# Three buffers instead of four for the raw weight panels of a two-layer trunk

## What is computed

```python
for layer in range(2):
    mod = silu(c) @ w_ada[layer] + b_ada[layer]            # six modulation vectors, for latents and context
    p = modulate(rms_norm(x, norm1), shift1, scale1) @ w_in[layer]
    y_m = mLSTM in both directions, context first, then latents
    y_a = grouped attention with 2-D rotary, latents see context and latents
    y_c = B * conv3(C * u)
    merged = sum over b of sigmoid(gate_b) * (y_b @ w_proj_b)
    x = x + g1 * (merged @ w_out)
    x = x + g2 * (relu(modulate(rms_norm(x, norm2), shift2, scale2) @ w_up) ** 2 @ w_down)
    # the context goes through the same, except behind the projections of the last layer
return rms_norm(x_latents) * final_norm
```

## Time and profile before

| | us |
|---|---|
| median of 3 runs | 1849.48 (1849.16 to 1849.73) |
| the profiled execution: its time | 1851.07 |
| the profiled execution: its span | 1849.3 |
| PE busy in the span | 1819.4 |
| DVE, ACT, POOL busy | 1051.0, 688.7, 156.6 |
| mean granted clock of TensorE | 0.997 |

### The profile page before, as it was taken

How to read it: one execution, slowest core, us unless ns; L and a number is a source line. 1 busy time by engine, 2 the same in 40 slices (tenths; PEclk the granted TensorE clock), 3 DMA queues, 4 the chain that set the end, 5 groups by cost and what they waited for, 6 DMA issues and landing times.

```text
span 1849.3 us, 24538 instructions
## 1 busy us (share of the span) xinstructions
PE 1819.4 (98%) x10027; PEld 1544.7 (84%) x10027; DVE 1051.0 (57%) x1544; ACT 688.7 (37%) x948; POOL 156.6 (8%) x159
## 2 busy tenths in 40 slices
PE   7999999999999999999999999999999999999998
PEld 4787788778888888878888888788998899999997
DVE  5435634544556665567675645655546656566555
ACT  3424434323222222243232323343644434445444
POOL 2100100001110101320000000301100110020000
PEclk9999999999999999999999999999999999999999
DMA  9221122121443453626444436132232375575653
GB/s 325 98 91 46 38 88 66 60 69 46 137 143 131 137 176 120 220 77 204 136 137 137 160 118 196 56 132 92 62 122 91 115 228 183 183 228 165 194 188 114
DMA packets 214271, 245.51 MB, mean 133 GB/s; under 512 B 5820, under 2 KB 186384, under 8 KB 214160
## 3 DMA queue, kind: packets, MB, share of 16 engines
q1 hardware_dynamic: 213856, 243.85, 40.8%
q10 hardware_dynamic: 304, 0.10, 0.0%
HBM read 242.89 MB, written 1.05 MB: 132 GB/s over the span
## 4 chain that ended last, share of the span: by engine, by line
PE 93%; DVE 2%; ACT 2%; issue 1%; POOL 0%; DVEq 0%; ACTq 0%; POOLq 0%
PE pp L1163 19%; PE pp L1167 19%; PE pp L1164 19%; PE pp L1172 4%; PE pp L1170 4%; PE pp L1171 4%; PE pc L1356 3%; PE pc L1408 2%; PE pp L1094 2%; PE pp L1095 2%; PE pp L1096 2%; PE pc L1053 2%; PE pc L1055 2%; PE pc L1054 2%; PE pc L1446 1%; PE pc L1423 1%
## 5 line engine op out<-in xcount | busy, mean ns | idle before, releaser
L1883 DVE TENSOR_TENSOR wL<-raw,wH 128x1024 fp32r<-128x1024 f32 (+1 forms) x360 | 452.5, 1298 | 238.6 <-ACT wH L1460 235.6
L1163 PE MATMUL pp<-hH,wH 128*128 128x512 f32 (+1 forms) x1708 | 571.1, 345 | 0.3 <-ACT hH L1668 0.3
L1164 PE MATMUL pp<-hH,wL 128*128 128x512 f32 (+1 forms) x1708 | 561.0, 339 | 0.0
L1460 ACT ACTIVATE wH<-raw 128x1024 fp32r<-128x1024 f32 x360 | 360.3, 1049 | 305.8 <-PE pp L1172 103.3
L1167 PE MATMUL pp<-hL,wH 128*128 128x512 f32 (+1 forms) x1708 | 439.7, 339 | 0.9 <-POOL hL L1856 0.6
L1163 PEld LDWEIGHTS pp<-hH,wH 128*128 128x128 f32 x1708 | 324.1, 190 | 43.4 <-issue 9.0
L1164 PEld LDWEIGHTS pp<-hH,wL 128*128 128x128 f32 x1708 | 324.3, 190 | 35.8 <-issue 1.7
L1167 PEld LDWEIGHTS pp<-hL,wH 128*128 128x128 f32 x1708 | 294.7, 190 | 36.7 <-POOL hL L1856 0.8
L1163 PE MATMUL pp<-yH,wH 128*128 128x512 f32 (+1 forms) x320 | 115.4, 367 | 0.0
L1170 PE MATMUL pp<-yH,wH 128*128 128x512 f32 (+1 forms) x320 | 114.4, 358 | 0.0
L1171 PE MATMUL pp<-yL,wH 128*128 128x512 f32 (+1 forms) x320 | 114.4, 358 | 0.0
(11 more groups left out here) (269 smaller groups left out, 2226.0 us busy)
## 6 DMA issues: line engine op xcount, KB each, us to landing
raw<-in_w_in SPq DMA_DIRECT2D x84, 1024.0 KB, 5.2
raw<-in_w_up SPq DMA_DIRECT2D x32, 1024.0 KB, 5.5
raw<-in_w_down SPq DMA_DIRECT2D x32, 1024.0 KB, 5.1
pair_W<-in_w_ada SPq DMA_DIRECT2D x10, 2048.0 KB, 8.0
ada_Y<-in_w_ada SPq DMA_DIRECT2D x10, 1024.0 KB, 11.9
ada_H<-in_w_ada SPq DMA_DIRECT2D x8, 1024.0 KB, 11.1
raw<-in_w_proj_m SPq DMA_DIRECT2D x8, 1024.0 KB, 5.1
raw<-in_w_proj_a SPq DMA_DIRECT2D x8, 1024.0 KB, 5.2
```

The costliest lines, as they stand in the source:

```text
L1163: pe.matmul(dsts[b], wh[b], hi[:, kt, ts_], start=first, stop=False)
L1164: pe.matmul(dsts[b], wl[b], hi[:, kt, ts_], start=False, stop=False)
L1460: act.activation(wH[:, p % HIGH, a:a + KH, :], raw[:, p % RAW, a:a + KH, :], ACT.Copy).then_inc(wH_ready, 1)
L1883: dve.tensor_tensor(wL[:, p % RAW, ks, :], raw[:, p % RAW, ks, :], wH[:, p % HIGH, ks, :].bitcast(F32), ALU.subtract).then_inc(wL_ready, 1)
```

## The change

The number of raw buffers goes from four to three.

```diff
-RAW = 4
+RAW = 3
```

## The result

The changed kernel takes 1856.6 us (median of 7 executions, 1854.34 to 1860.09), the kernel before 1849.73 (7 executions, 1848.45 to 1850.82). The ratio is 1.0041, with a 95% interval from 1.0031 to 1.0050: slower, by 5.7 to 9.2 us. The forecast was 1857.2. The profiled execution took 1858.86 us, its span is 1857.1.

What follows compares the result with a forecast made beforehand. PE was taken to bound the kernel, its work plus its standing still. Place A 1.9, place B 2.8 and clock 3.0 sum to 7.7 us on the median of 1849.48, giving 1857.2 us; range 1851.5 to 1862.0.

Steps and rivals of the forecast that it cites:

- What bounds the kernel, and no new work: Time is PE's work plus its standing still; the change adds no work and costs only what it adds to those.
- ACT waits for the transfer, and this is hidden nearly everywhere: About 5.3 us of waiting on ACT per panel, costing PE nothing where it has a further panel to do.
- First layer, attention and the end of the program: Drains in the first layer and attention, and the output work at the end: no cost; first layer bounds 0 and +1 us.
- Place A: Last projection: PE's wait for hL grows as the drain stands behind panel 145's subtractions; 1.9 us, from +1.4 to +2.2.
- Place B: Last wo panel, 147: residual late behind panel 149's subtractions, PE waits for the sum of squares; 2.8 us.
- The clock, 3.0 us: One fall to half clock behind each of the two long PE waits, 1.5 us each; bounds 0 and 3.3 us.
- The clock holds: Rival: the waits at the last projection and last wo panel without clock falls, 4.7 us, time 1854.2; chance 0.18.
- Not slower: Rival: loads land fast enough or PE's waits hide in steps taken as chained, 1849.5 to 1853 us; chance 0.22.
- The margin breaks: Rival: lateness carries over between some 60 short panels, PE waits in each, 12 us more, 1869; chance 0.11.
- the 3.9 us that the weights have left: Last layer's short panels: margin between the first weight half being ready, 7.6 us, and PE's need at 11.5 us.
- the 2 us that I had found for the drains: Last layer: DVE's drains come 3.0 us late, with about 2 us left before the slot is asked for again.

Runs made afterwards that it cites:

- `two_late`: Kernel before, four raw buffers kept, with only the loads of panels 145 and 149 waiting for the end of panel p - 3: 1855.66 us, ratio 1.0038.
- `four_late`: Kernel before, four raw buffers and memory layout kept, with every load waiting for the end of panel p - 3: 1858.04 us, ratio 1.0046.

## Why the prediction was right

- **What bounds the kernel, and no new work.** Right. The instructions are the same, PE's idle time rose by 4.1 us and its busy time by 3.7. One reading was short: besides the waits of 1.2 and 0.6 us the last layer has one of 1.35 us at its first panels (1183.22, before and after), which changes nothing in the sum.
- **ACT waits for the transfer, and this is hidden nearly everywhere.** Right: over 118 waits, two of them felt by PE. First layer, attention and the end of the program cost nothing, since the shift between the traces moves there only with the clock. PE never waits for wL.
- **Place A, 1.9 us.** Measured 1.8. I had put it down to hL alone (line 1856). The trace has 1.8 us for hH, which I had not named as a wait, and the old 0.6 us for hL behind it. Both hang on the same drain, so the sum held and the label didn't. Within the sum two small errors nearly cancel, which is luck: 145 took 5.0 us to land and not 5.3, and the two subtractions, which met POOL's last hL, took 3.06 us, 0.7 more than undisturbed, where I had added 0.5. `two_late` gives 1.2 us to the load of 145 and leaves 0.6, which I put down to that of 144.
- **Place B, 2.8 us.** Measured 3.0 as a shift, 2.77 as a wait. The landing took 5.5 us (1650.48 to 1655.96), not 5.3, which accounts for the 0.2 us between my number and the shift.
- **The clock, 3.0 us.** 2.8 us by the mean clock of many executions. In the one profile it is 4.6 us behind A and B, and there two falls elsewhere are missing. The term was right as a mean; as a statement on each place it was not. Behind B the clock was at half for twice as long as I took in this profile and not at all in that of `four_late`; behind A it stayed up in that of `two_late` (waits of 1.2 and 0.6 us). That the median came within 0.6 us of the forecast is luck as well: the seven executions lie between 1854.3 and 1860.1 us.
- **The rivals.** "The clock holds" is excluded by the windows behind A and B and by the mean clock of the executions. "Not slower" is out: the loads of 144, 145, 148 and 149 took 5.0 to 5.5 us to land. "The margin breaks" did not happen with three buffers, but I had worked out its point from the wrong margin. I put it at 9.2 us of landing, by the 3.9 us that the weights have left; the 2 us that I had found for the drains would put it near 7.3. Two buffers are like a landing 5.76 us later, beyond either point. There the largest waits of PE are for small work, and the row for weights is a twentieth of the idle time. Where between 5.5 and 11 us the loss begins is not shown.

## What to carry to other kernels

A buffer that is taken away moves a transfer from behind a panel to the front of whatever is queued behind the instruction that waits for it. Look for the places where the busiest engine has no next panel to go on with. As long as the lateness stays below the slack everywhere else, it shows only there, nearly at its full size. Here the clock added about half as much again in the mean of the executions (2.8 us on 4.8 us of waits), and anything from nothing to 3.2 us at one place in one profile. Do not take a slack measured on one consumer (the weights) as the slack of all: count it for each thing that stands behind the same waiting instruction.

## What the runs showed of the hardware

**DVE and POOL take turns.** In the prediction I wrote that the rows can't tell a lock from sharing. Read instruction by instruction, they can. POOL's and DVE's single instructions at place A in the kernel before:

```profile
1626.09 1.30 POOL L1856 TENSOR_TENSOR hL<-merged,hH 128x512 fp32r<-128x512 f32 x1 [5.18 <-ACT hH L1755]
```

```profile
1628.04 1.70 DVE L1883 TENSOR_TENSOR wL<-raw,wH 128x1024 fp32r<-128x1024 f32 x1 [4.91 <-ACT wH L1460]
```

```profile
1628.60 2.29 POOL L1856 TENSOR_TENSOR hL<-merged,hH 128x512 fp32r<-128x512 f32 x1
```

Undisturbed, POOL's takes 1.3 us, and one subtraction of DVE 1.2 us. POOL's second one ended at 1628.65, and DVE's, which had begun in the midst of it, at 1629.74, 1.1 us later. POOL's third began at 1628.60 and ended at 1630.89, 1.15 us behind DVE's end; DVE's second ended at 1631.97, 1.1 us behind that. Each ends one undisturbed duration, less a little, behind the end of the other's (the profile's spans on POOL are rough, but DVE's, of 1.70 and 2.31 us instead of 1.2, say the same). The Trainium skill (SBUF — State Buffer, two separate sides) states of the port pair that DVE and GpSimd share that whichever starts first holds it for the whole instruction, and that the other is blocked. The rows agree, and they add that DVE's subtractions get their turn between POOL's instructions and need not wait for the last of them.

**The clock does not fall at each wait of a given length.** Behind the same wait of 1.11 us near 812 the clock was at half in the profile of the kernel before and at full in that of the changed kernel. Among the kernels with three or four buffers eleven profiles have this wait unfilled, and three of them show the fall. Behind the wait of 1.2 us near 1391 it is four of twelve, behind that of 1.35 us near 1183 none of eleven. At B it fell in the changed kernel behind 2.8 us and did not in `four_late` behind 2.9. The Trainium skill (TensorE: Matmul & The Clock Gate, Part 1) says of a kernel's start that the number of slow matmuls differs between runs of the same kernel; the rows show the like behind waits in its midst. In the changed kernel's seven executions times from 1854.3 to 1860.1 us go with mean clocks from 0.998 to 0.994.
